# Decode memory attention in a hybrid decoder step: four heads of a sequence in column groups of TensorE

## The reference, cut to what matters

```
def mem_branch(p, mk, mv, dtype):            # group C: 4 heads x 128, 256 memory tokens
    q = p['mem_q'].reshape(B, L, MEM_H, MEM_DH).astype(F32)
    s = jnp.einsum('blhd,bmhd->bhlm', q, mk.astype(F32)) * (MEM_DH ** -0.5)
    a = jax.nn.softmax(s, axis=-1)
    o = jnp.einsum('bhlm,bmhd->blhd', a, mv.astype(F32)).reshape(B, L, MEM_W)
    return (o * jax.nn.silu(p['mem_z'].astype(F32))).astype(dtype)
...
c_s = mem_branch(ps, c_mk, c_mv, x_s.dtype)  # B = 8, L = 4, c_mk and c_mv (8, 256, 4, 128)
```

## Time and profile before

| | |
|---|---|
| median of 3 runs | 3161.3 us (3156.34 to 3163.57) |
| profiled execution: its own time | 3160.96 us |
| its span (first to last instruction) | 3159.3 us |
| TensorE matmul busy | 2960.0 us, 94% of the span |
| mean granted TensorE clock | 0.967 of full |
| head of `attend_bc` | 2241.05 to 2310.72 us, 69.7 us |
| slots 0 to 5 | 2310.7 to 2340.4 us |

### The profile page before, as it was taken

How to read it: one execution, slowest core, us unless ns; L and a number is a source line. 1 busy time by engine, 2 the same in 40 slices (tenths; PEclk the granted TensorE clock), 3 DMA queues, 4 the chain that set the end, 5 groups by cost and what they waited for, 6 DMA issues and landing times. The chain is left out here.

```text
span 3159.3 us, 36093 instructions
## 1 busy us (share of the span) xinstructions
PE 2960.0 (94%) x13209; PEld 1763.6 (56%) x13209; DVE 1399.6 (44%) x2480; ACT 451.4 (14%) x970; POOL 404.3 (13%) x567
## 2 busy tenths in 40 slices
PE   6899999999999969999999999999689999499998
PEld 5578888888644424444444444444445565255553
DVE  3141111111112123899999998655232231144553
ACT  2110000000011114400000110000222231122221
POOL 0000000000012110000000000066003200133332
PEclk9999999999999989899999999999899999699999
DMA  6322112211434242301202322266454412746642
GB/s 214 81 78 61 57 53 76 78 51 54 147 114 163 81 155 105 127 20 71 78 17 74 134 69 102 76 198 216 163 188 145 128 45 83 226 125 194 194 140 97
DMA packets 248895, 353.59 MB, mean 112 GB/s; under 512 B 42412, under 2 KB 164756, under 8 KB 243484
## 3 DMA queue, kind: packets, MB, share of 16 engines
q1 hardware_dynamic: 207436, 269.86, 26.4%
q0 software_dynamic: 14784, 61.88, 6.2%
q10 hardware_dynamic: 26544, 20.08, 2.2%
HBM read 267.86 MB, written 86.43 MB: 112 GB/s over the span
## 5 line engine op out<-in xcount | busy, mean ns | idle before, releaser
L276 PE MATMUL sbank<-w,xT 128*128 128x512 f32 x2048 | 884.0, 594 | 6.6 <-ACTq L227 2.9
L276 PEld LDWEIGHTS sbank<-w,xT 128*128 128x128 f32 x2048 | 389.5, 191 | 497.2 <-issue 490.2
L1062 PE MATMUL bank<-w,xT 128*128 128x512 f32 (+1 forms) x768 | 295.5, 540 | 0.0
L1126 PE MATMUL bank<-w,xT 128*128 128x256 f32 x1152 | 253.9, 380 | 0.0
L1126 PEld LDWEIGHTS bank<-w,xT 128*128 128x128 f32 x1152 | 217.8, 190 | 30.3
L1922 PE MATMUL at_bank_bc<-w,at_hT 128*128 128x512 f32 x512 | 230.0, 593 | 3.9 <-ACT at_bc_out L2080 3.9
L1062 PEld LDWEIGHTS bank<-w,xT 128*128 128x128 f32 x768 | 145.2, 193 | 124.3 <-issue 109.2
L1126 PE MATMUL bank<-w,area 128*128 128x256 f32 x960 | 212.1, 379 | 0.0
L894 DVE TENSOR_TENSOR pout<-pout,bank 128x256 f32<-128x256 f32 x120 | 50.5, 421 | 339.5 <-PE bank L1126 339.5
L1126 PEld LDWEIGHTS bank<-w,area 128*128 128x128 f32 x960 | 182.4, 190 | 24.8
L1568 DVE MATCH_REPLACE8 area<-m,area 128x384 f32<-128x384 f32 (+2 forms) x192 | 165.8, 877 | 0.0
(11 more groups left out here) (383 smaller groups left out, 3294.7 us busy)
## 6 DMA issues: line engine op xcount, KB each, us to landing
w<-in_w_in SPq DMA_DIRECT2D x18, 2048.0 KB, 10.2
w<-in_w_in SPq DMA_DIRECT2D x28, 1024.0 KB, 5.3
area<-in_x_prompt SPq DMA_DIRECT2D x16, 1024.0 KB, 7.5
proj<-pout_b SPq DMA_DIRECT2D x64, 256.0 KB
proj<-pout SPq DMA_DIRECT2D x96, 128.0 KB, 1.7
headT<-area ACTq DMA_DIRECT2D x8, 1024.0 KB, 9.4
area<-roped_q_of_decode POOLq DMA_DIRECT2D x32, 256.0 KB
w<-in_w_out SPq DMA_DIRECT2D x4, 2048.0 KB, 15.7
```

What stands on the lines that cost most here:

```text
L276: last = k.nc.tensor.matmul(bank[0:r, 0:self.w], k.xT[:, c, r0:r0 + r], k.w[:, u, c, 0:self.w], start=c == 0, stop=c == KT - 1)
L1062: last = nc.tensor.matmul(dst[:, 0:wd], k.xT[:, c, t * P:(t + 1) * P], wc, start=c == 0, stop=c == KT - 1)
L1126: last = nc.tensor.matmul(bank[t][:, 0:256], x(c, t), at[name][:, c, :], start=first and c == 0, stop=c == 7, skip_group_check=True)
```

## The change: what it does

- The keys' loop is replaced by a straight run over 8 sequences. For a sequence TensorE does 8 transposes into two banks (5 and 6, or 2 and 3, taking turns); ScalarE copies one bank (128x512), VectorE the other; then four matmuls, one for each head, with 32 query columns each into 32 partitions of bank 4 of their own.
- The queries are laid out once: `dmq_of` is cleared, and one copy places them at a step of 36 columns, so that the 32 columns taken at 32 b hold the 4 queries of sequence b in the rows of sequence b and zeros elsewhere. `pz`, `zero` and the `empty` matmuls go.
- Keys of sequences 2 to 4 get buffers of their own in free room of `k.w` and are loaded at the stage's start; 5 to 7 wait for a buffer that was turned.
- The selected keys' softmax is cut up and put between the steps of the memory keys' softmax; its banks change to 0, 1 and 3. Its input `vn` has a semaphore of its own and is waited for in slot 23.
- The memory probabilities are put into `spread` by two copies straight from PSUM, and the values' product is 64 matmuls of 32 columns by 128 value columns, four heads side by side. `own_head` of this result is one plain copy. `spread` is then overwritten with the selected keys' probabilities.
- Rows of the result are head-major, so its store is four DMAs instead of one. `mv` moves in SP's queue behind the last values.

```diff
-            for dst, src in ((kn, k.kn4), (vn, k.vn4)):
-                for t in range(DEC_T):
-                    sp.dma_start(dst[:, t, :], ...).then_inc(small_in, 16)
-            sp.dma_start(mv[:, :, :], ...).then_inc(mv_in, 16)
-            with sp.Fori(1, DEC_B // 2) as i:
-                for u in range(2):
-                    sp.wait_ge(mkd_free, i * 2 + u + 1)
-                    sp.dma_start(mkd[:, u, :, :], ...).then_inc(mkd_in[u], 16)
+            sp.dma_start(dmq[:, :, :], ...).then_inc(dmq_in, 16)        # now first of all
+            for b in range(2, 5):
+                load_mkd(b)
+            ... nid, hm, qr, kn ...
+            for b in range(5, DEC_B):
+                sp.wait_ge(mkd_turned, b - 4)
+                load_mkd(b)
+            ... vn, mvd of 5 to 7, mv, load(0), load(1) ...
 
# TensorE
+            def turn_mkd(b):
+                if b < 2:
+                    pe.wait_ge(mkd_in[b], 16)
+                else:
+                    pe.wait_ge(mkd_late[b - 2], 16)
+                    pe.wait_ge(mkd_kept_a, b - 1)
+                    pe.wait_ge(mkd_kept_v, b - 1)
+                for h in range(H):
+                    for c in range(2):
+                        last = nc.tensor.transpose(
+                            bank[(5, 2)[b % 2] + h // 2][:, N_MEM * (h % 2) + P * c:N_MEM * (h % 2) + P * (c + 1)],
+                            mkd[b % 5][:, c, h * DH:(h + 1) * DH], k.ident[:])
+                last.then_inc(mkd_turned, 1)
+            def dots_mkd(b):
+                pe.wait_ge(mkd_kept_a, b + 1)
+                pe.wait_ge(mkd_kept_v, b + 1)
+                for h in range(H):
+                    last = nc.tensor.matmul(bank[4][NS * h:NS * (h + 1), 0:N_MEM], dmq_of[:, h, NS * b:NS * (b + 1)],
+                                            mkdT[:, b % 2, h, :], start=b == 0, stop=b == DEC_B - 1)
+                last.then_inc(mdots, 1)
+            turn_mkd(0)
+            pe.wait_ge(dmq_set, 2)
+            for b in range(DEC_B):
+                if b + 1 < DEC_B:
+                    turn_mkd(b + 1)
+                dots_mkd(b)
             pe.wait_ge(lk_ready, 1)
             ... lk's two transposes and the one-column matmuls, now into banks 0 and 1 ...
-            (the loop with turn(n), the matmul by pz, and the empty matmuls)
             pe.wait_ge(pm_ready, 1)
             ... pmd's two transposes ...
+            pe.wait_ge(pd_ready, 1)
+            ... pd's two transposes, into bank 3 ...
             pe.wait_ge(mvd_in, 16 * DEC_B)
-            for n in range(N_C):
-                pe.wait_ge(pz_ready, n + 1)
-                nc.tensor.matmul(bank[6][:, :], pz[:, n % 4, :], mvd[:, n, :], start=False, stop=False,
-                                 skip_group_check=True).then_inc(pz_used, 1)
+            pe.wait_ge(pm_spread, 2)
+            for b in range(DEC_B):
+                for c in range(2):
+                    for h in range(H):
+                        last = nc.tensor.matmul(bank[6][NS * h:NS * (h + 1), 0:DH], spread[:, c, h, NS * b:NS * (b + 1)],
+                                                mvd[:, 2 * b + c, h * DH:(h + 1) * DH], start=b + c == 0,
+                                                stop=b == DEC_B - 1 and c == 1)
+            last.then_inc(closed, 1)
 
# ScalarE: one 128x512 copy for each sequence; the first exponential is now pmd's, pd's comes after it
# VectorE: memset dmq_of, place dmq, keep_mkd(0..3), memset spread, keep_mkd(4), (5), lk and eq, keep_mkd(6),
#          nprod and eqh, keep_mkd(7), nd, then
+            dve.wait_ge(mdots, DEC_B)
+            ... maximum of bank 4 and its scale -> pm_max ...
             dve.wait_ge(lk_turned, 1)
+            ... nbias, lt ...
+            dve.wait_ge(pm_exp, 1)
+            ... normalise pmd -> pm_ready; rest of lt and its maximum -> pd_max ...
+            dve.wait_ge(pm_turned, 1)
+            for c in range(2):
+                set_spread(c, bank[5][:, c * P:(c + 1) * P], pm_spread)
             dve.wait_ge(pd_exp, 1)
             ... normalise pd -> pd_ready, keep pdT ...
+            dve.wait_ge(closed, 1)
+            nc.vector.tensor_copy(oc[:], bank[6][:, 0:DH]).then_inc(out_ready, 1)
+            dve.wait_ge(out_ready, 1)
+            dve.sem_inc(dec_clear, 1)
+            for c in range(2):
+                set_spread(c, pdT[:, c, :], masks)
-            own_head(oc, bank[6])
```

More of the change, by code:

```diff
@@ L1662, in attend_bc @@
         S("dec_p_spread"))
[L1663 to L1667, removed]
+    mkd_late, dmq_in, dmq_set = k.sems("dec_memk_late", DEC_B - 2), S("dec_mq_loaded"), S("dec_mq_spread")
+    mkd_turned, mkd_kept_a, mkd_kept_v, mdots = (
+        S("dec_memk_turned"), S("dec_memk_by_act"), S("dec_memk_by_dve"), S("dec_mem_dots"))
+    pm_max, pm_exp, pm_ready, pm_turned, pm_spread = (
+        S("dec_mem_max"), S("dec_mem_exp"), S("dec_mem_p"), S("dec_mem_p_turned"), S("dec_mem_p_spread"))
+    dec_clear, closed, vn_in = S("dec_banks_read"), S("dec_sum_closed"), S("dec_new_v_loaded")
     v_in, quad_done = k.queue_sems("v_gathered", 8), S("dec_quad_done")
@@ L1827, in _ @@
             last.then_inc(mk_turned, 1)
+            def turn_mkd(b):
[24 more added lines that the diff above has]
+                dots_mkd(b)
             pe.wait_ge(lk_ready, 1)
+            pe.wait_ge(mk_kept, 2)
             for c in range(2):
-                nc.tensor.transpose(bank[2][:, c * P:(c + 1) * P], lk[:, c, :], k.ident[:])
+                nc.tensor.transpose(bank[0][:, c * P:(c + 1) * P], lk[:, c, :], k.ident[:])
             for n in range(DEC_T):
-                last = nc.tensor.matmul(bank[3][:, n:n + 1],
+                last = nc.tensor.matmul(bank[1][:, n:n + 1],
                                         eqh[:, NS * n:NS * (n + 1), :].rearrange("p a b -> p (a b)"),
@@ L1836, in _ @@
             last.then_inc(lk_turned, 1)
[L1837 to L1870, removed]
-                    nc.tensor.matmul(bank[4][:, 0:N_MEM], pz[:, n % 2, :], mkdT[:, n % 2, :], start=False,
-                                     stop=False, skip_group_check=True).then_inc(mdots, 1)
-            empty(bank[4][:, 0:N_MEM], mkd[:, 0, 0, 0:N_MEM], False).then_inc(mdots, 1)
             pe.wait_ge(pm_ready, 1)
-            pe.wait_ge(mkd_kept, 2 + DEC_B * H)
+            pe.wait_ge(mkd_kept_a, DEC_B)
+            pe.wait_ge(mkd_kept_v, DEC_B)
             for c in range(2):
@@ L2102, in _, with keep_mkd @@
             order = Order(dve, order_sem)
-            for ap, value in ((ones, 1.0), (zero, 0.0)):
-                order(nc.vector.memset(ap[:], value))
+            nc.vector.memset(dmq_of[:], 0.0).then_inc(dmq_set, 1)
+            order(nc.vector.memset(ones[:], 1.0))
+            dve.wait_ge(dmq_in, 16)
+            dve.wait_ge(dmq_set, 1)
+            nc.vector.tensor_copy(dmq_of[:, :, :].rearrange("p h (b x) -> p h b x", x=36)[:, :, :, 0:DEC_T],
+                                  dmq[:, :, :].rearrange("p h (b t) -> p h b t", t=DEC_T)).then_inc(dmq_set, 1)
+            def keep_mkd(b):
+                dve.wait_ge(mkd_turned, b + 1)
+                if b >= 2:
+                    dve.wait_ge(mdots, b - 1)
+                nc.vector.tensor_copy(mkdT[:, b % 2, 2:4, :].rearrange("p a b -> p (a b)"), bank[(5, 2)[b % 2] + 1][:, :]
+                                      ).then_inc(mkd_kept_v, 1)
+            for b in range(4):
+                keep_mkd(b)
             nc.vector.memset(spread[:], 0.0).then_inc(masks, 1)
-            dve.wait_ge(small_in, 16 * (4 + 2 * DEC_T))
+            keep_mkd(4)
+            keep_mkd(5)
+            dve.wait_ge(small_in, 16 * (3 + DEC_T))
             for c in range(2):
@@ L2168, in own_head @@
                                                               dst[:], ALU.mult, ALU.add))
-            dve.wait_ge(closed, 1)
-            own_head(oc, bank[6])
-            dve.sem_inc(out_ready, 1)
-            dve.sem_inc(dec_clear, 1)
             def keep(s):
@@ L2236, in _ @@
                     own_head(ob, dec)
+                    dve.wait_ge(vn_in, 16 * DEC_T)
                     for n in range(DEC_T):
```

97 lines of the change are left out of this document (43 added, 54 removed).

## The result

The changed kernel takes 3122.94 us (median of 4 runs, 3116.52 to 3124.91) against 3159.24 us before (4 runs): ratio 0.9878, 95% interval 0.986 to 0.9896. The forecast was 3127, the range 3118 to 3137. The profiled execution took 3123.22 us by itself, its span is 3121.5 us.

What follows compares the result with a forecast made beforehand. TensorE, 94% busy, was taken to bind, with the head serial. Terms 21.0 + 2.9 + 5.5 + 6.0 + 0.7 give 36.1 us instead of 69.7, 33.6 less than 3161: forecast 3127 us, range 3118 to 3137.

Steps and rivals of the forecast that it cites:

- last keys landed: Head, keys' loads: the last keys arrive about +21 us behind the stage's start, bounds +17.3 and +26.6.
- behind them, to the last dots: Head, after the last keys land: 8 transposes, copy and dots take 2.9 us (2.2 at full clock, 3.4 at half).
- both softmaxes: Head, from the last dots to the value product: memory and selected keys' softmaxes take 5.5 us, bounds 4.9 and 6.2.
- value product: Head, 64 value matmuls: 6.0 us, starting at half clock and recovering on the way (3.70 full, 7.4 half).
- end: Head, from the value product to slot 0: 0.7 us, where it was 1.77.
- half-clock rival: TensorE at half clock all through the head, softmax 6.2, values 7.4, slots 2 us longer: about 3132 us; chance 0.20.
- Transfers bind more: Rival for the head's loads: all queues share the poorest rate, keys at +26.6, total about 3133 us; chance 0.12.
- Better on both: Rival for the head: keys at +17.3 and full clock, head 28.8 us, total 3120 us; chance 0.15.
- Column groups: Dots and values: expected four side by side; the rival that they don't overlap adds 13 us, 3140; chance 0.05.
- The switch of modes: Keys' part: going in and out of column groups once per sequence costs TensorE about 0.14 us.
- The table load: ScalarE, between the eighth key copy and the first exponential: adds nothing, up to 0.3 us if the gap is shorter.
- What follows: Slots behind the head move along with slot 0; the clock over slots 0 to 5 gives plus 2 or minus 3 us.

Runs made afterwards that it cites:

- the gates: Changed kernel with GpSimd's first gather held until all eight sequences' keys are turned, or until the value product ends: head 29.39 or 29.66 us, against 36.50.
- dots_wide: Changed kernel with the keys' dots at full width, queries 128 columns wide and zero-filled, no column groups: head 38.55 us, total 3136.59 us (one run).
- changed_timed: The changed kernel unaltered, timed and profiled again: median 3127.1 us of 5 runs, ratio to before 0.9886, head 35.58 us.
- fill_the_wait: Changed kernel plus seven unused matmuls behind sequence 3's dots, where TensorE waited for keys: head 35.53 us, total 3123.45 us (one run).
- warm_head: Changed kernel with gathers held until the value product ends, plus short unused matmuls at three TensorE waits: head 27.33 us, total 3124.81 us (6 runs).
- the head gate: Changed kernel with GpSimd's first gather held until the value product ends, profiled twice: head 29.66 and 28.17 us.
- values_wide: Changed kernel with the old full-width value product, its zero matmuls and four head copies: head 49.49 us, total 3138.36 us (one run).
- softmax_first: Changed kernel with the selected keys' softmax put back ahead of the memory keys: head 46.35 us, total 3133.62 us (one run).
- gathers_behind_keys: Changed kernel with GpSimd's first gather held until all eight sequences' keys are turned: head 29.39 us, total 3115.95 us (one run).
- head_gate_timed: Changed kernel with gathers held until the value product ends, timed: median 3120.31 us of 4 runs, ratio to before 0.9868; head 28.17 us.

## Why the prediction was right, point by point

The sum was 36.1 us for the head; it took 36.50 and 35.58. Term by term, by the first profile:

| step | forecast | measured |
|---|---|---|
| last keys landed | +21.0 | +21.0 |
| behind them, to the last dots | 2.9 | 5.5 |
| both softmaxes | 5.5 | 4.63 |
| value product | 6.0 | 4.82 |
| end | 0.7 | 0.54 |
| sum | 36.1 | 36.50 |

- **The keys' arrival** binds, as said: the gates show it from one side, `dots_wide` from the other. The last keys came when the forecast had them (+20.4 in `changed_timed`). The step behind them was too small by 2.6 us, because it supposed that TensorE would be up to date by then and have one sequence left. It wasn't. The keys of sequences 5, 6 and 7 came within 2.8 us of each other, and at half clock TensorE needs 2.9 us for one; when the last landed it was only about to turn sequence 6. Kept at clock 1.00 in `fill_the_wait`, the last dots end 24.67 us behind the stage's start instead of 26.51, so most of the 2.6 us is the clock and the rest the second sequence.
- **Luck in the sum.** The three terms behind the dots were together 2.2 us too large, the two softmaxes even below their bound of 4.9, and that hides the 2.6. The total has luck in it too: the head, slots 0 to 5 and the rest together are 33.4 us shorter, nearly the forecast's 33.6; that the two spans differ by 37.8 is the earlier start of the stage, which the change doesn't make. The 1.90 us by which the stretch from slot 6 on is longer lie within the scatter of the changed kernels (817.7 in `warm_head`, 823.5 in `changed_timed`).
- **The half-clock rival** (0.20) was half right: the clock did fall in the key wait (0.55 in a microsecond near its end, 0.70 over the last three sequences), and `fill_the_wait` prices this at 2.2 us. It didn't stay down: 0.89 in the softmax chain, 0.78 in the value product.
- **Transfers bind more** (0.12): no; the last keys were there at +21.0, and the bound of +26.6 wasn't reached. **Better on both** (0.15): its 28.8 us is what the head gate gives (28.17, 29.66), but not the change alone.
- **Column groups** do work side by side, for 32 columns by 128 (0.029 us per record at clock 1.00) and by 256 (eight records step by 0.57 us, where one after the other they would take 1.7). The switch of modes: transposes and dots step by 0.49, 0.53 and 0.57 us, in all 1.59; in `dots_wide`, which never leaves full width, the same transposes step by 0.44 twice. With 0.43 for the dots themselves that is 1.31, so in and out costs 0.28 us per sequence, twice the 0.14 that I took from the earlier trace rows. The Trainium skill (TensorEngine Tiling (Array Packing), "Key Properties") says that a change of the tiling mode drains TensorE; the trace agrees in so far as the change isn't free. Over eight sequences it is 2.2 us of TensorE's time, in part under the key waits.
- **The value product** was taken at a clock between the levels, and so it was (0.78). `values_wide` gives 13.0 us for this part of the change, the largest piece that one edit moves.
- **The table load** costs nothing, as the sum had it:

```profile
2262.12 1.28 ACT L2041 ACT_TABLE_LOAD   x1
2263.96 0.47 ACT L2041 ACTIVATE at_pmd<-at_bank_turn,at_dec_stats 128x256 f32<-128x256 f32 x1 [0.55 <-DVE at_dec_stats L2152]
```

  It ends at 2263.40; the exponential follows 0.56 us later, released by its bias from VectorE. The Trainium skill (ScalarE: Activation LUTs, "What ACT_TABLE_LOAD costs") gives a drain of about 1.4 us beside the load, which by an estimate would have put the exponential at 2264.8; here it began at 2263.96, and the measurement decides.
- **What follows** moved along: slots 0 to 5 by 2.17 us in the direction of a better clock (0.88 for 0.77), inside the plus 2 and minus 3; `load(0)` was there before `dec_clear`.

How the saving of 33 us splits: the value product and its end 13.0 (`values_wide`), the order of the softmaxes 9.9 (`softmax_first`), the column groups of the dots 2.1 (`dots_wide`), a second copier none. The rest, about 8 us if these add up (33.2 - 24.9), wasn't taken apart: presumably it lies with the loop over pairs of heads, its slots of queries and its short buffers, but no run shows this.

## What to carry to other kernels

When a serial stretch loses TensorE work, work out afresh what arrives last: here the keys' loads, and what lengthened them stood on another engine's queue and wasn't urgent. Don't suppose that only the last piece stands behind the last arrival: here three pieces landed within 2.8 us of each other, faster than TensorE could work them off. And price that work at the clock that TensorE will have after the wait. A gain of 7 us in a profile's own stretch can be invisible in a kernel whose totals scatter by 10.

## What the runs showed of the hardware

- **Two queues, one set of engines.** A load of 512 KB landed in 3.6 us (median) before, when it was issued with no gathers beside it; in 10.2 with three such loads issued at a time and eight gathers in flight; in 5.9 with the gathers held back. SP's own issue slowed too: four loads of `vn` took it 6.24 us, in `gathers_behind_keys` 2.80. The Trainium skill (DMA: Bandwidth & Descriptors, "Queues, rings and completion order") says that each DMA engine takes turns between its queues packet by packet; the landing times agree with a share that the gathers take from the large loads.
- **The clock gives and takes.** Slots 0 to 5, the same instructions each time, took 25.40 us at clock 1.00 (`fill_the_wait`), 27.55 at 0.88, 28.51 at 0.82 and 29.50 at 0.77 (`warm_head`), as 29.72 at 0.77 before. One profile is off this line, `head_gate_timed` with 32.06 at 0.79: it has the step of 7.25 us shown above. The scatter of these slots, 25.4 to 32.1 us, is as large as what the gates bring in the head.
- **Drift upstream.** Ahead of the stage the code is the same in all runs, and its time lies within 13.5 us. That is more than all gates and fillings bring, and what makes it was not looked for.
